# Sums of squares of the gating heads: one float32 ones matmul, or two float32r ones matmuls on a high and a low part

## The reference

```python
scores = jnp.einsum("bnthd,bnshd->bnhts", q_dec, k_dec) * causal
o_intra = jnp.einsum("bnhts,bnshe->bnthe", scores, v)
# o_inter: a scan over chunks with state = decay * state + k_end^T v
o = (o_intra + jnp.moveaxis(o_inter, 0, 1)).reshape(bsz, seq, HG_HEADS, HG_DV)
o = _rms_norm(o, o_g...)          # x * rsqrt(mean(x * x) + 1e-6) * g, over each head's 128 columns
o = o * jax.nn.silu(g_raw)
```

## Time and profile before

| what | value |
|---|---|
| median of 3 runs | 3015.84 us (3015.79 to 3016.53) |
| the profiled execution's own time | 3017.09 us |
| its span, first to last instruction | 3015.3 us |
| mean granted clock of TensorE | 0.997 of full speed |
| instructions | 41624 |
| mean rate of the DMA engines | 89 GB/s |

### The profile page before, as it was taken

One profiled execution on the slowest core, in us unless ns is written; L12 is line 12 of the kernel. 1 busy time (PEld: TensorE's weight loads), 2 busy tenths in 40 slices (PEclk: granted clock), 3 DMA queues, 4 the chain that ended last, 5 costly groups with the idle time before them and its releaser, 6 DMA issues.

```text
span 3015.3 us, 41624 instructions
## 1 busy us (share of the span) xinstructions
PE 2983.2 (99%) x14092; PEld 2431.1 (81%) x14092; DVE 1734.2 (58%) x2641; ACT 1167.8 (39%) x1746; POOL 1410.8 (47%) x1040
## 2 busy tenths in 40 slices
PE   8999999999999999999999999999999999999998
PEld 6888888877888888888887788878888888788886
DVE  7986677774524598568677634367772243611214
ACT  4233333464332424333336533236553333422223
POOL 5443443455455543444344555543443545454544
PEclk9999999999999999999999999999999999999999
DMA  4222222212222322222221222221222322222222
GB/s 150 98 71 77 89 83 80 81 43 93 95 98 100 126 91 84 84 90 70 83 88 47 77 99 98 98 91 63 77 77 91 106 87 100 89 100 97 92 98 90
DMA packets 73272, 267.90 MB, mean 89 GB/s; under 512 B 8128, under 2 KB 9024, under 8 KB 72768
## 3 DMA queue, kind: packets, MB, share of 16 engines
q1 hardware_dynamic: 70560, 254.84, 24.5%
q10 hardware_dynamic: 2592, 11.46, 1.0%
HBM read 262.07 MB, written 4.19 MB: 88 GB/s over the span
## 4 chain that ended last, share of the span: by engine, by line
PE 86%; issue 7%; POOL 5%; DVE 1%; ACT 1%; DVEq 0%; ACTq 0%; POOLq 0%
PE gem L366 19%; PE gem L368 19%; PE gem L367 19%; POOL wlo L299 5%; PE gem L759 2%; PE gem L761 2%; PE gem L760 2%; PE gem L486 2%; PE gem L487 2%; PE gem L485 2%; PE gem L602 2%; PE gem L625 1%; PE xp L661 1%; PE gem L604 1%; PE gem L603 1%
## 5 line engine op out<-in xcount | busy, mean ns | idle before, releaser
L299 POOL TENSOR_TENSOR wlo<-raw,whi 128x512 fp32r<-128x512 f32 x956 | 1315.2, 1398 | 1540.8 <-ACT whi L921 1540.8
L921 ACT ACTIVATE whi<-raw 128x1024 fp32r<-128x1024 f32 x478 | 504.6, 1057 | 680.9 <-PE gem L368 512.6
L366 PE MATMUL gem<-zhi,whi 128*128 128x512 f32 x1680 | 658.4, 392 | 0.3 <-DVE zlo L1541 0.3
L368 PE MATMUL gem<-zhi,wlo 128*128 128x512 f32 x1680 | 653.9, 389 | 0.0
L367 PE MATMUL gem<-zlo,whi 128*128 128x512 f32 x1680 | 653.6, 389 | 0.0
L366 PE MATMUL gem<-hhi,whi 128*128 128x512 f32 x1296 | 507.6, 392 | 0.0
L368 PE MATMUL gem<-hhi,wlo 128*128 128x512 f32 x1296 | 504.4, 389 | 0.0
L367 PE MATMUL gem<-hlo,whi 128*128 128x512 f32 x1296 | 504.2, 389 | 0.0
L366 PEld LDWEIGHTS gem<-zhi,whi 128*128 128x128 f32 x1680 | 315.4, 188 | 67.6 <-issue 2.2
L367 PEld LDWEIGHTS gem<-zlo,whi 128*128 128x128 f32 x1680 | 315.5, 188 | 66.6 <-issue 1.7
L368 PEld LDWEIGHTS gem<-zhi,wlo 128*128 128x128 f32 x1680 | 315.3, 188 | 66.0
(11 more groups left out here) (363 smaller groups left out, 4228.6 us busy)
## 6 DMA issues: line engine op xcount, KB each, us to landing
raw<-in_slabs SPq DMA_DIRECT2D x478, 512.0 KB, 3.5
U<-in_x SPq DMA_DIRECT2D x4, 512.0 KB, 8.0
U<-in_x ACTq DMA_DIRECT2D x1, 2048.0 KB, 9.7
xsave<-U ACTq DMA_DIRECT2D x1, 2048.0 KB, 8.2
U<-xsave ACTq DMA_DIRECT2D x1, 2048.0 KB, 8.4
out_y<-yr SPq DMA_DIRECT2D x8, 256.0 KB, 2.2
tab<-in_tab_ret ACTq DMA_DIRECT2D x2, 512.0 KB, 8.5
tab<-in_tab_att ACTq DMA_DIRECT2D x2, 512.0 KB, 3.7
```

Of the source, the lines that this page charges most:

```text
L299: part = pool.tensor_tensor(wlo[:, k % 4, c], raw[:, k % 2, c], whi[:, k % 4, c].bitcast(f32), O.subtract)
L366: pe.matmul(o, wh, hi, start=(n == 0), stop=False)
L368: mm = pe.matmul(o, wl, hi, start=False, stop=(n == len(terms) - 1))
L921: act.activation(whi[:, k % 4, :], raw[:, k % 2, :], A.Copy).then_inc(hi_done, 1)
```

## The change

The sum of squares of a head becomes two float32r matmuls of `ones_r`, on the high and the low part of the squares. ACT squares twice from PSUM (to `OSQ` in float32 and to the float32r tile `hhi[7]`), and then copies to `OH`. DVE makes the low part (`square_low`) after the first product of `k_levels`, and PE waits for its new semaphore `hg_low` in place of `hg_osq`. The place of the matmuls among PE's rows, `cuts[4]`, goes from 27, 24, 22, 20, 23 to 28, 26, 24, 23, 25 (heads 0, 1, 2, 3 to 6, 7).

```diff
--- before.py
+++ after.py
@@ -246,7 +246,7 @@
         klev_ready, lev_ready = sem("klev_ready"), sem("lev_ready")
         hg_t, hg_tr, hg_sc, hg_sel, hg_p, hg_up, hg_inter = (sem(n) for n in (
             "hg_t", "hg_tr", "hg_sc", "hg_sel", "hg_p", "hg_up", "hg_inter"))
-        hg_osq, hg_var, hg_rstd = sem("hg_osq"), sem("hg_var"), sem("hg_rstd")
+        hg_osq, hg_low, hg_var, hg_rstd = sem("hg_osq"), sem("hg_low"), sem("hg_var"), sem("hg_rstd")
         ones_ready = sem("ones_ready")
 
         merged_in, merged_hi = sem("merged_in"), sem("merged_hi")
@@ -812,17 +812,18 @@
                                    skip_group_check=True)
                 mm.then_inc(hg_inter, 1)
                 rows(cuts[3], cuts[4])
-                pe.wait_ge(hg_osq, p + 1)
-                pe.matmul(xp[:, 2, :], ones[:, :], OSQ, start=True, stop=True).then_inc(hg_var, 1)
+                pe.wait_ge(hg_low, p + 1)
+                pe.matmul(xp[:, 2, :], ones_r[:, :], zhi[:, 7, :], start=True, stop=False)
+                pe.matmul(xp[:, 2, :], ones_r[:, :], zlo[:, 7, :], start=False, stop=True).then_inc(hg_var, 1)
                 rows(cuts[4], 32)
 
-            head_products(0, BLOCK_G + 1, BLOCK_U + 1, (14, 16, 18, 23, 27))
-            head_products(1, BLOCK_G + 2, BLOCK_U + 2, (0, 11, 15, 19, 24))
-            head_products(2, BLOCK_G + 3, BLOCK_U + 3, (0, 9, 13, 17, 22))
+            head_products(0, BLOCK_G + 1, BLOCK_U + 1, (14, 16, 18, 23, 28))
+            head_products(1, BLOCK_G + 2, BLOCK_U + 2, (0, 11, 15, 19, 26))
+            head_products(2, BLOCK_G + 3, BLOCK_U + 3, (0, 9, 13, 17, 24))
             with pe.Fori(3, 7) as p:
-                head_products(p, BLOCK_G + 1 + p, BLOCK_U + 1 + p, (0, 6, 11, 15, 20))
+                head_products(p, BLOCK_G + 1 + p, BLOCK_U + 1 + p, (0, 6, 11, 15, 23))
             Gv, uv = BLOCK_G + GM_V, BLOCK_U + GM_V
-            head_products(7, Gv, uv, (0, 6, 11, 15, 23))
+            head_products(7, Gv, uv, (0, 6, 11, 15, 25))
             for k in range(4, 8):
                 hslab(Gv, k, uv)
             Go, uo = BLOCK_G + HG_OUT, BLOCK_U + HG_OUT
@@ -1386,9 +1387,9 @@
                 act.wait_ge(hg_inter, p + 1)
 
                 act.wait_ge(z_ready, DEPTH * 40 + p + PRIMED)
+                act.activation(OSQ, xp[:, 3, :], A.Square)
+                act.activation(Z[DEPTH][0][:, 7, :], xp[:, 3, :], A.Square).then_inc(hg_osq, 1)
                 act.activation(OH, xp[:, 3, :], A.Copy)
-                act.drain()
-                act.activation(OSQ, OH, A.Square).then_inc(hg_osq, 1)
                 act.wait_ge(hg_var, p + 1)
                 inv_sqrt(RS, xp[:, 2, :], P, EPS, hg_rstd)
 
@@ -2170,7 +2171,12 @@
                 return tt(dst.rearrange("p (a b) -> p a b", a=n), src.rearrange("p (a b) -> p a b", a=n),
                           factor[:, :, None].to_broadcast([P, n, T // n]), O.mult)
 
-            def k_levels():
+            def square_low(p):
+
+                dve.wait_ge(hg_osq, p + 1)
+                tt(zlo[:, 7, :], OSQ, zhi[:, 7, :].bitcast(f32), O.subtract).then_inc(hg_low, 1)
+
+            def k_levels(p=None):
 
                 dve.tensor_copy(DEC[16], chunks(EB)[:, :, CHUNK16 - 1])
                 dve.drain()
@@ -2181,6 +2187,8 @@
                     tt(DEC[2 * w], half(DEC[w], 0), half(DEC[w], 1), O.mult)
                     dve.drain()
                     last = longer(KES[2 * w], KES[w], KF[w])
+                    if w == 16 and p is not None:
+                        square_low(p)
                 last.then_inc(klev_ready, 1)
 
             def el_q(hd):
@@ -2243,12 +2251,13 @@
                 update(p)
                 el_scan(hd)
                 el_k(hd)
-                k_levels()
+                k_levels(p)
                 head_end(p)
                 el_q(hd)
                 dve.drain()
             select(7)
             update(7)
+            square_low(7)
             head_end(7)
             dve.drain()
 
```

## The result

The changed kernel is slightly slower: ratio 1.0015 to the kernel before, 95% interval 1.0009 to 1.0021, some 4.5 us by the ratio, 2.7 to 6.3 by its interval. Medians: 3021.47 us against 3016.45 us, each of 22 runs (one of the changed kernel's, 6255.08, was disturbed and is left out of the ratio; the others lie between 3019.33 and 3022.09). The forecast was 3019.0 in a range of 3013.5 to 3023.0, and within 0.2% of before.

What follows compares the result with a forecast made beforehand. PE, busy 99% of the span, was taken to bound the kernel. Saving -3.2, waits for the low part +1.26 and stalls at the scores +5.11 gave +3.2 us: 3019.0 us, range 3013.5 to 3023.0.

Steps and rivals of the forecast that it cites:

- PE's saving: Sum of squares on PE: two float32r matmuls replace one float32 sum, 0.40 us less a head, -3.2 us over 8 heads.
- ACT's third activation: Two squares and a copy on ACT, about 0.6 us more, hidden in its wait for `hg_var`.
- The subtraction: DVE's `square_low` behind the first product of `k_levels`: 0.69 us with POOL silent, high end 1.72.
- The rule of the Trainium skill: GpSimd contends with VectorE's two-SBUF-input instructions; by that rule alone the subtraction could cost 1.03 us more in seven heads.
- The stalls: PE waits for `hg_low` in heads 0 to 2, +1.26 us, and for the next head's scores from heads 0 to 6, +5.11 us.
- the loop from the sum to the scores: From the pair's start through inverse root, `head_end` and levels to the next head's scores on PE: 12.25 us.
- The 0.67: Time from the second step of ACT's inverse root to DVE's line 2233, where ACT alone releases it: 0.67 us.
- rival 1: DVE's levels finish ahead of POOL, loop shorter by 1.0 us or more, saving arrives: 3013.7 us, chance 0.17.
- rival 2: The float32r pair costs no less than the single sum, through weight loads or format switch: 3019.4 us, chance 0.07.
- Rival 3: POOL's next slab falls into the last level, one more turn of 1.03 us in 7 heads: 3026.2 us, chance 0.08.
- My bound of 0.8 us for that room: Between the last level's start at 7.02 after POOL's first and the next slab's earliest POOL start, 7.8: 0.8 us.

Runs made afterwards that it cites:

- numbers 3 and 7: Changed kernel: 3 at sum's old places without the low part, 3012.95 us; 7 with scores two rows later, heads 0 and 1's sum one row later, 3013.26 us.
- number 5: Changed kernel with ScalarE reading the queries out of PSUM before copying the slab, so POOL starts later: 3019.81 us, ratio 1.0011 to the kernel before.

## Why the prediction was right, and where its sizes were off

**PE's saving** held: the pair takes 0.47 for 0.86, and it comes through as 0.40 to 0.42 a head where nothing stalls (numbers 3 and 7).

**ACT's third activation** is hidden, as said. In the timeline of ACT in head 4 the three start 0.48 us apart, closer than the 0.6 that I took; ACT is then idle for 3.00 us until `hg_var` comes.

**The subtraction** took 0.68 to 0.69, POOL being silent. The rule of the Trainium skill that was weighed (GPSIMD Engine Reference, Specifications: contention with VectorE instructions that have two SBUF inputs) holds at the split and the levels, 1.6 to 1.8 us where 0.69 is their own, and it does not touch an instruction that runs while POOL is idle: the added time a head by that rule alone, 1.03, did not come.

**The stalls** came where they were forecast. By step, added time between the scores: forecast 1.02, 0.45, 1.02, then 0.27 four times; measured, end to end, 1.14, 0.54, 1.16, then 0.37, 0.41, 0.41, 0.38. Each step is 0.09 to 0.14 longer than forecast, and the eight heads together cost +4.05 where +3.2 was forecast. The term that was too small is the loop from the sum to the scores, 12.25 by my rows and 12.37 by the profile after. Its parts in head 4: the pair to the inverse root 0.66 where I took 0.72 from the retention; the two steps of the root 0.76, as taken; the exponential to line 2233 of before 0.77 where I took 0.67; `head_end` and the levels 10.03 (2202.55 + 0.70 - 2193.22) where I took 9.94; from there 0.15 where I took 0.16, of which 0.11 is the stall inside the scores.

The 0.67 was read in head 7, and head 7 is not like the others. In the first seven heads, which stand in a loop of VectorE's program, its sequencer runs a register instruction in front of this line; in the eighth it does not. The view of that line in the changed kernel:

```profile
L2241 DVE SCALAR_TENSOR_TENSOR U<-U,vec x8: 750/752/753, 2078.5 to 2282.3; 128x512 f32<-128x512 f32 x8
L2241 DVEq FUSED_REGOPS  x7: 57/57/65, 2078.4 to 2251.7; - x7
```

In the chain of head 4 it takes 0.06 with 0.05 of issue behind it, which is about the 0.10 that I was short. In the kernel before this was out of sight, since DVE was not ready sooner there. It fits the order at the split too. VectorE came there 3.12 us after the exponential instead of 3.02, POOL 3.09 after it; so POOL was first by 0.03, and the split took 1.80 where I had the 1.72 of before.

**The total.** The median is 2.5 us above the forecast of 3019.0. The heads are 0.9 of it; 0.6 is the median of before, 3015.84 in the three runs that I had and 3016.45 in all 22; for the remaining 1.0 I have no cause, and it is within the scatter of the runs.

**The rivals.** The saving did not arrive (rival 1): the lead over POOL did not come, and number 5, which made one, gained 1.3 us and not the saving. The pair is cheaper, as said against rival 2, whose time of 3019.4 is too close to mine for the median to tell the two apart; numbers 3 and 7 do. Rival 3's extra POOL turn did not come: after the change, POOL's next slab starts at 2203.56, 0.3 us after the last level of head 4, and its copy waited for its DMA, as the rows of head 0 had it. My bound of 0.8 us for that room was measured from the start of the last level and stands at 1.0 (2203.56 - 2202.55).

## What to carry to other kernels

When work is placed between rows of a long matmul stream, its place is one end of a loop through other engines: moving it later to cover a wait in front takes the same time from the wait behind. Add up the loop from the moved instruction to the place where PE needs its result before choosing, and if there is no room, move that place too; here two rows at the scores of heads 1 to 7, with one more at the sum of heads 0 and 1, turned a loss of 4.5 us into a gain of 3. Test it by moving the places alone in the old kernel, which separates the places from the arithmetic. And where a cost is read from the first or the last of several like pieces, look whether it is built like the rest: the 0.10 us that go with one register instruction, missed in this way, were the largest part of the error of each head.

## What the runs showed of the hardware that I had not expected

VectorE and POOL, both with 128x512 operations of two SBUF inputs, go at the same pace while both have work: POOL's four instructions take 1.60 us each (6.39), VectorE's 1.6 to 1.8, where alone VectorE's take 0.69 and POOL's 1.25 to 1.28. That fits turns instruction by instruction. Tiny instructions of VectorE seem to wait for whole ones of POOL too. In the kernel before, timelines of DVE and POOL in head 4:

```profile
2184.01 1.25 DVE L2179 COPY U<-U 128x16 f32<-128x16 f32 x1
2185.18 0.16 DVE L2180 COPY U<-U 128x16 f32<-128x16 f32 x1
2185.25 1.27 DVE L2181 TENSOR_TENSOR U<-U 128x16 f32<-128x16 f32 x1
...
2183.94 2.56 POOL L299 TENSOR_TENSOR wlo<-raw,whi 128x512 fp32r<-128x512 f32 x2 [10.28 <-ACT whi L921]
```

Two of the three small ones last as long as an instruction of POOL and end with it; the one between them takes its own 0.16.

Giving VectorE the first turn (number 5) changes which of its instructions waits, and hardly how long the sequence takes. From the start of the split to the end of the last level, with the product of `el_q` at line 2197 between them, it is 7.68 us in the changed kernel (2195.57 to 2203.25) and 7.49 in number 5 (2196.37 to 2203.86).

And consecutive activations from PSUM of 128x512 with no bias started only 0.48 us apart, though each is shown with 0.59 to 0.61.
